# Down projection in block products of seven for five of six pieces, with GpSimd splitting its operands

## The reference

```python
D_MODEL = 1024
SEQ = 1024
D_FF = 3 * D_MODEL
...
def conv_ffn(h, w_up, conv_w, conv_b, w_down):
    u = dwconv(h @ w_up, conv_w, conv_b, FFN_CONV_W // 2)
    a, v = jnp.split(u, 2, axis=-1)
    return (jax.nn.gelu(a) * v) @ w_down
...
        x = x + g2 * conv_ffn(hx2, w_up[l], ffn_conv_w[l], ffn_conv_b[l], w_down[l])
```

## Time and profile before

| | us |
|---|---|
| median of 3 runs | 1796.97 |
| lowest and highest run | 1795.78, 1797.33 |
| span of the profiled execution, first to last instruction | 1793.2 |
| median less span | 3.8 |
| TensorE busy | 1759.5 |
| VectorE busy | 1217.6 |
| ScalarE busy | 716.4 |
| GpSimd busy | 551.6 |

### The profile page before, as it was taken

One profiled execution on the slowest core, in us unless ns is written; L12 is line 12 of the kernel. 1 busy time (PEld: TensorE's weight loads), 2 busy tenths in 40 slices (PEclk: granted clock), 3 DMA queues, 4 the chain that ended last, 5 costly groups with the idle time before them and its releaser, 6 DMA issues.

```text
span 1793.2 us, 23179 instructions
## 1 busy us (share of the span) xinstructions
PE 1759.5 (98%) x8348; PEld 1467.8 (82%) x8348; DVE 1217.6 (68%) x1377; ACT 716.4 (40%) x918; POOL 551.6 (31%) x261
## 2 busy tenths in 40 slices
PE   7999999999999999999999999999999999999998
PEld 5897888888788789877888878888888888888887
DVE  7978666669516487878217379999989988514425
ACT  5335556566101188840002135444444444302205
POOL 1036666766345476635446710000000000000000
PEclk9999999999999999999999999999999999999999
DMA  9230111111344200057215512222122224523212
GB/s 372 68 112 27 58 60 50 50 50 46 136 149 159 70 1 0 1 178 255 83 58 201 167 43 94 94 82 94 73 82 91 82 84 163 191 97 127 68 36 94
DMA packets 55570, 176.90 MB, mean 99 GB/s; under 512 B 11730, under 2 KB 12114, under 8 KB 54868
## 3 DMA queue, kind: packets, MB, share of 16 engines
q1 hardware_dynamic: 46388, 147.22, 23.2%
q10 hardware_dynamic: 9120, 28.84, 5.0%
HBM read 139.86 MB, written 30.93 MB: 95 GB/s over the span
## 4 chain that ended last, share of the span: by engine, by line
PE 82%; DVE 10%; DMA 4%; issue 2%; ACT 2%; SPq 0%; POOL 0%; ACTq 0%; DVEq 0%; POOLq 0%
PE acc L900 16%; PE acc L901 16%; PE acc L902 16%; PE gp L900 10%; PE gp L901 10%; PE gp L902 10%; DVE wg L2391 2%; PE acc L1196 1%; DMA wg<-in_mod_rest 1%; DVE wgr L2391 1%; DMA wst<-in_w_in 1%; DMA wgr<-in_mod_rest 1%; DVE hx_lo L2254 1%; DVE y_lo L2254 1%; DVE T_lo L2524 0%
## 5 line engine op out<-in xcount | busy, mean ns | idle before, releaser
L900 PE MATMUL acc<-hx_hi,whi_both 128*128 128x512 f32 x672 | 263.0, 391 | 3.4 <-ACT sg L1404 1.5
L901 PE MATMUL acc<-hx_lo,whi_both 128*128 128x512 f32 x672 | 261.9, 390 | 0.0
L902 PE MATMUL acc<-hx_hi,wlo_both 128*128 128x512 f32 x672 | 261.7, 389 | 0.0
L726 POOL TENSOR_TENSOR whi_both<-wst,ones 128x1024 fp32r<-128x1024 f32 x57 | 149.8, 2628 | 258.7 <-PE acc L902 230.2
L728 POOL TENSOR_TENSOR wlo_both<-wst,whi_both 128x1024 fp32r<-128x1024 f32 x57 | 178.3, 3129 | 4.5
L900 PEld LDWEIGHTS acc<-hx_hi,whi_both 128*128 128x128 f32 x672 | 126.2, 188 | 32.9 <-ACT sg L1404 2.7
L902 PEld LDWEIGHTS acc<-hx_hi,wlo_both 128*128 128x128 f32 x672 | 126.2, 188 | 26.6
L901 PEld LDWEIGHTS acc<-hx_lo,whi_both 128*128 128x128 f32 x672 | 126.3, 188 | 25.1
L900 PE MATMUL acc<-T_hi,fac_hi 128*128 128x512 f32 x264 | 102.9, 390 | 0.3 <-DVE fac_lo L2563 0.3
L902 PE MATMUL acc<-T_hi,fac_lo 128*128 128x512 f32 x264 | 102.8, 389 | 0.0
L901 PE MATMUL acc<-T_lo,fac_hi 128*128 128x512 f32 x264 | 102.7, 389 | 0.0
(11 more groups left out here) (385 smaller groups left out, 4647.3 us busy)
## 6 DMA issues: line engine op xcount, KB each, us to landing
wst<-in_w_in SPq DMA_DIRECT2D x43, 512.0 KB, 3.5
wst<-in_w_up SPq DMA_DIRECT2D x26, 512.0 KB, 4.1
wg<-in_mod_rest ACTq DMA_DIRECT2D x24, 512.0 KB, 5.0
ffn_row_scratch<-ca SPq DMA_DIRECT2D x24, 512.0 KB, 2.6
wst<-in_w_down SPq DMA_DIRECT2D x32, 384.0 KB, 3.1
g_in<-ffn_row_scratch SPq DMA_DIRECT2D x24, 512.0 KB, 7.4
wup<-in_w_up SPq DMA_DIRECT2D x22, 512.0 KB, 4.1
wmod<-in_mod_first SPq DMA_DIRECT2D x16, 512.0 KB, 15.3
```

The source lines that it names most:

```text
L726: nc.gpsimd.tensor_tensor(whi[s][:, 0:kc, :], wst[s][:, 0:kc, :], ones_of(kc), mult).then_inc(S["w_hi"], 1)
L900: mm(out_ap, w_h, x_h, start=first, stop=False)
L901: mm(out_ap, w_h, x_l, start=False, stop=False)
L902: return mm(out_ap, w_l, x_h, start=False, stop=last)
```

## The change

The down projection now takes four rows at a time (`ROWS`), in five fast pieces and one plain one. In a fast piece, each pair of result blocks (four pairs, `r` = 0 to 19 over all pieces) is made from seven block products (`down_product`, 6 matmuls each) in place of eight. That needs:

- **On GpSimd, in the up projection:** five operations on half rows for each two steps (`even_row`, `odd_row`) that make the sums of operand blocks, which SyncE stores in `ffn_sum_scratch`; ScalarE's next `centre_of` waits until they are read (`turn_read`).
- **On SyncE:** seven operand loads of 512 KB per fast piece (`load_operand`), four in the plain one, instead of six rows per piece; weights in loads of 512 KB (`load_dn(r)`), of which number 3 stands behind the store of row 23.
- **On ScalarE:** the high parts `op_hi` and, per pair, seven of 256 columns (`df_hi`).
- **On VectorE:** four weight block sums per pair (`weight_rows`), seven low parts (`dn_low`), and each product out of PSUM into one of 28 running totals (`add_product`; a copy in the first piece). The taps and the product of row 23 stand in pairs 0 and 1.
- **On GpSimd, in the down projection:** all low parts of operands from the second piece on (`operand_low`; of the first piece three of seven), and seven additions per pair that turn the totals into result blocks (`join`), which VectorE then adds to the residual (`mix_rows`, four per pair).
- **In the tail:** all first transposes stand behind the last matmul of the plain piece, and ScalarE's five remaining `plain_high_of` stand ahead of its first square.

```diff
+            def down_product(s):
+                j, n, f = s // (NF * PAIRS), s // NF % PAIRS, s % NF
+                pe.wait_ge(S["dn_ready"], AT["dn_ready"] + s + 1)
+                if n == 0:
+                    op_ready(pe, j, f)
+                if s >= 8:
+                    pe.wait_ge(S["dn_total"], AT["dn_total"] + s - 7)
...
+                for k in range(KAP):
+                    last = three(dn_bank(s), df_hi[f][:, k, :], df_lo[f][:, k, :], op_hi[j % 2][f][:, k, :],
+                                 op_lo[j % 2][f][:, k, :], k == 0, k == KAP - 1)
+                last.then_inc(S["dn_full"], 1)
...
+            def odd_row(t):
...
+                nc.gpsimd.tensor_tensor(turn[2][:, :], ca[:, HALF:SEQ], turn[0][:, :], sub).then_inc(S["turn_made"], 1)
...
+                nc.gpsimd.tensor_tensor(turn[1][:, :], ca[:, HALF:SEQ], turn[1][:, :], sub).then_inc(S["turn_made"], 1)
...
+                nc.gpsimd.tensor_tensor(turn[0][:, :], ca[:, 0:HALF], turn[2][:, :], sub).then_inc(S["turn_made"], 1)
...
+            for r in range(FAST * PAIRS):
+                j, n = divmod(r, PAIRS)
+                if n:
+                    for f in (2 * n - 2, 2 * n - 1) + ((6,) if n == PAIRS - 1 else ()):
+                        if f in op_of(j + 1) and low_by_pool(j + 1, f):
+                            operand_low(j + 1, f)
+                if j == FAST - 1 and n:
+                    join(n - 1)
+            join(PAIRS - 1)
...
+                for f in range(NF):
+                    add_product(NF * r + f)
+                    if f == 0 and r + 1 < FAST * PAIRS:
+                        weight_rows(r + 1)
+                    if r + 1 < FAST * PAIRS:
+                        dn_low(r + 1, f)
+                    elif f % 2 and f < 6:
+                        plain_low_of(f // 2)
+                    if r == 0 and f == 3:
+                        value_taps_of(FC - 1, uv)
+                    elif r == 1 and f == 1:
+                        taps_of(FC - 1, ug)
+                    elif r == 1 and f == 5:
+                        product_of(FC - 1)
...
+            load_dn(2)
+            store_row(FC - 1, 0)
+            sp.dma_start(x1t[6][:, :], x1_d[6]).then_inc(S["x1_loaded"], 16)
+            load_dn(3)
...
+            for m in range(3, KC):
+                plain_high_of(m)
```

More of the change, by code:

```diff
@@ L43 @@
 NWP = FC - 2
-PK = 6
-PIECES = FC // PK
-ND = PIECES * KC
+KAP = 2
+ROWS = 2 * KAP
+FAST = FC // ROWS - 1
+PAIRS = KC // 2
+NF = 7
+NPROD = FAST * PAIRS * NF
 NG = 4
@@ L272, in build @@
+    otile = [sb(f"otile{t}", otile_at[t], [P, D_MODEL]) for t in range(XT)]
     fncol = sb("fncol", HX + 32768, [P, KC])
@@ new lines, in up_step @@
+                store_row(e, i)
+                if isinstance(w, int) and w > FC - ROWS:
+                    return
+                if e == 1:
+                    store_odd(i)
+                else:
+                    store_even(i + 1)
+            wait(sp, S["turn_made"], AT["turn_made"] + 1)
+            store_turned(0, 0, 0)
+            up_pairs(sp, up_step)
+            for f, after in ((4, 3), (5, 3), (6, 4)):
+                sp.wait_ge(S["up_full"], AT["up_full"] + 7 * (NWP - 1) + after)
+                load_operand(0, f)
@@ L703, in _ @@
+            sp.wait_ge(S["dn_full"], AT["dn_full"] + NPROD - NF + 1)
+            sp.dma_start(x1t[7][:, :], x1_d[7]).then_inc(S["x1_loaded"], 16)
+            sp.wait_ge(S["dn_full"], AT["dn_full"] + NPROD - NF + 5)
+            sp.dma_start(fncol[:, :], D["final_norm_w"].rearrange("(k p) -> p k", p=P),
+                         allow_slow_non_contiguous=True).then_inc(S["fn_loaded"], 16)
+            for r in range(FAST * PAIRS + 2, FAST * PAIRS + PAIRS):
+                load_dn(r)
             for t in range(XT - 1):
@@ L891, in _, with even_row @@
             low_w(W_S6 + 1)
+            def even_row(t):
+                wait(pool, S["f_prod"], AT["f_prod"] + 2 * t + 1)
+                if isinstance(t, int) and t == 0:
+                    pool.wait_ge(S["t_lo"], AT["t_lo"] + 4)
+                else:
+                    wait(pool, S["turn_stored"], AT["turn_stored"] + 64 * t)
+                nc.gpsimd.tensor_tensor(turn[0][:, :], ca[:, HALF:SEQ], ca[:, 0:HALF], sub).then_inc(S["turn_made"], 1)
+                nc.gpsimd.tensor_scalar(turn[1][:, :], ca[:, HALF:SEQ], 1.0, None, mult).then_inc(S["turn_read"], 1)
@@ new lines, in operand_low, with join @@
+            def operand_low(j, f):
+                pool.wait_ge(S["f_hi_s"], AT["f_hi_s"] + NF * j + f + 1)
+                nc.gpsimd.tensor_tensor(op_lo[j % 2][f][:, :, :], op_in[j % 2][f][:, :, :], op_hi[j % 2][f][:, :, :], sub)\
+                    .then_inc(S["op_lo_pool"], 1)
+            def join(n):
+                t, step = total[n], NF * n
+                pool.wait_ge(S["dn_total"], AT["dn_total"] + NPROD - NF * PAIRS + NF * (n + 1))
+                for a, b, o, after in ((0, 1, 1, 0), (0, 4, 4, 0), (1, 2, 2, 1), (1, 3, 1, 3), (2, 5, 5, 3), (1, 6, 6, 4), (2, 3, 3, 4)):
+                    if after:
+                        pool.wait_ge(S["e_done"], AT["e_done"] + step + after)
+                    nc.gpsimd.tensor_tensor(t[o][:, :], t[a][:, :], t[b][:, :], add).then_inc(S["e_done"], 1)
@@ new lines, in up_step @@
+            def up_step(e, i):
+                w = 2 * i + e
+                if isinstance(w, int) and w > FC - ROWS:
+                    return
+                if e == 1:
+                    odd_row(i)
+                else:
+                    even_row(i + 1)
+            even_row(0)
+            up_pairs(pool, up_step)
+            for f in range(3):
+                operand_low(0, f)
+            for r in range(FAST * PAIRS):
[6 more added lines that the diff above has]
+                    join(n - 1)
@@ new lines, in mix_rows @@
+            def mix_rows(n):
+                dve.wait_ge(S["e_done"], AT["e_done"] + NF * n + NF)
+                for m, blocks in ((2 * n, (4, 6)), (2 * n + 1, (5, 3))):
+                    for h in range(2):
+                        part = slice(HALF * h, HALF * (h + 1))
+                        v.scalar_tensor_tensor(out=x1t[m][:, part], in0=total[n][blocks[h]][:, :], scalar=rest[:, 3, m:m + 1],
+                                               in1=x1t[m][:, part], op0=mult, op1=add).then_inc(S["x1_mixed"], 1)
@@ L2655, in up_step @@
                 product_of(w)
+                if not more:
+                    weight_rows(0)
+                    for f in range(4):
+                        dn_low(0, f)
                 bottom_right(e, i)
@@ L2666, in up_step @@
                 else:
-                    g_low(0)
+                    operand_low(0, 3)
                 bottom_left(e, i)
```

417 lines of the change are left out of this document (253 added, 164 removed).

## The result

The changed kernel takes 1855.14 us (median of four runs, 1854.49 to 1855.20) against 1796.38 before (1795.39 to 1797.33): 1.0324 times as long, 95% interval 1.031 to 1.0339. The forecast was 1826 with a range of 1797 to 1850. The direction of the forecast was right and its time was not: the loss is twice the one predicted.

The account below looks back on a forecast made before the run. TensorE bounds the kernel before, VectorE the fast pieces after. Fast pieces 233 plus tail 73.7 make 306.7 us against 277.7, +29 (-27.2 matmuls, +42 waiting, +14 tail): span 1822, forecast 1826 us, range 1797 to 1850.

Parts of the forecast that it names:

- Term 1: TensorE, down projection: 1032 matmuls instead of 1152, 120 fewer at 0.227 us each, removing 27.2 us.
- Term 2: VectorE, fast pieces: additions, weight low parts and block sums cost 8.0 us per pair against TensorE's 9.5.
- Term 3: Fast pieces: each GpSimd operand low part holds out VectorE's two-SBUF-input reads, costing it 1.7 us (bounds 1.3 and 2.3).
- hidden: Rival, fast pieces: GpSimd's low parts fall into VectorE's waits and VectorE keeps up; 1787 us, chance 0.12 for 1777 to 1793.
- half: Rival: 1.3 us instead of 1.7 per GpSimd operation, no load wait or tail contention; 1804 us, chance 0.08 for 1793 to 1808.
- The sum of the fast pieces: Down projection's five fast pieces: VectorE-bound, 233 us instead of TensorE's 190.7, so 42 us of waiting.
- The up projection: GpSimd's half-row operations cost VectorE 3.1 us per two steps of 2.7 to spare; taken as 0 for TensorE.
- the passage: Between the up projection and the first down matmul: 0 us added.
- VectorE behind in the up projection too: Rival: slow `tensor_scalar` adds 8 us, plus heavier tail or longer-held sums; 1840 to 1850, chance 0.18 up to 1855.
- the likeliest case: VectorE bounds the fast pieces of the down projection; 1808 to 1840 us, chance 0.62.
- The tail: From last fast product to the end: 48.4 to the half-row addition, 6 of contention, 19.0 after; 73.7 us.
- Before the FFN: Stretch ahead of the FFN: 0 us added.

Follow-up runs that it names:

- the experiment: Changed kernel with GpSimd's operand low parts of pieces 1 to 5 replaced by fills with zeros, which read nothing (work left out): 1810.49 us.

## Why the prediction was wrong in size, step by step

- **Term 1 (matmuls, -27.2 us): right.** Four pairs take 38.1 us where nothing holds TensorE up.
- **Term 2 (VectorE 8.0 us per pair): right.** The estimate was 0.335 us to the next start for 256 columns; a low part of line L2789 starts at 1610.93 and the next operation at 1611.27, 0.34 us later, and pieces with 39.9 us busy fit 8.0.
- **Term 3 (1.7 us per low part on GpSimd): right as a mechanism and as a number.** 1.5 us in the changed kernel, 1.7 where VectorE has no other waits. The additions out of PSUM kept 0.68. The "hidden" and "half" rivals fall. The Trainium skill's rule ("SBUF — State Buffer", Who interferes with whom) fits what the down projection shows: the subtraction contends with VectorE's two-input reads, VectorE's PSUM reads are left alone, and so, by the experiment, is everything beside a fill. The subtractions keep VectorE out for their whole length, as term 3 said. The `tensor_scalar` of 1.50 us in the up projection, beside which VectorE lost 0.30, does not, so which operations meet does not yet say for how long.
- **The sum of the fast pieces (233, measured 250.0): the first failed step.** It took ScalarE and SyncE as free. I had followed each moved instruction into GpSimd's and VectorE's streams, but not the operand loads into SyncE's, where they stand behind a weight load that a late VectorE releases; that put 12.0 us of waits on VectorE. The wait for the weight load of pair 3 was 2.3 over the 3 us, VectorE's start 2.4 over the 5 us; the smaller 1.5 per low part gives 6 back. Some 6 us more, in pieces 0 and 4, I can't split: with short low parts those two still take 49.4 and 45.6 us, and all the stretches at half clock lie there (0.95 granted over the fast pieces, where the prediction left the clock at 1.00).
- **The up projection (0, measured 9.2) and the passage (0, measured 4.9): the second failed step, nearly as large.** The budget was computed as 0.4 us over per pair of steps and then set to zero, since the factors are ready 6 us ahead. Ahead helps once; ten pairs over by 0.4 already use 4 of those 6 us, and the real 0.93 leaves a wait in each pair. Missing in the budget was ScalarE's 0.85 us, which before the change comes up in nine steps and after it in twenty; on the other side, the `tensor_scalar` was priced 0.6 too high. The rival "VectorE behind in the up projection too" was the one that came true, but by that wait and not by a slow `tensor_scalar`, and on top of the likeliest case, not instead of it.
- **The tail (73.7, measured 70.9).** Its terms as written, 48.4 + 6 + 19.0, make 73.4. The squares came as computed. The 6 us for contention between joins and `mix_rows` did not reach the half-row addition (48.9 us against 48.4 without them): `mix_rows` is held out by about as much, 17.50 us for the sixteen where eight of them undisturbed take 5.38, but in time that VectorE has. Then the tail lost 3 us that were not foreseen: from there to the end it is 22.0 instead of 19.0, with TensorE's granted clock at half for 10 us around its 7.40 us wait. That these errors partly cancel is luck.
- **Before the FFN (0, measured 2.8):** not the change (last section).
- **The range** left out the sum of two cases that each had a place in it. They were treated as alternatives; they add.

## What to carry to other kernels

Before moving an elementwise operation with two on-chip inputs from VectorE to GpSimd, look at what VectorE reads meanwhile. Here it read two such inputs half of the time: each moved operation cost it 1.5 to 1.7 us, and doing it itself cost 1.13. Before taking a budget that is a little over as zero, multiply it by the number of steps, and put every engine's in-order waits in it, ScalarE's and the DMA queue's too: an engine that runs late releases its buffers late, and so delays what feeds it. A removed wait is worth its length only if nothing was running for free under it (17.3 us removed and 10.4 won with low parts on GpSimd, 13.4 removed and 13.7 won without).
